# Load order of the down weights, place of the norm row, and order of the mixer's last group in a two-layer streaming encoder

## The chip, the cores and the metric

The kernel runs on one core of one Trainium2 chip. The metric is the device time of one execution in microseconds (us). A core has TensorE (matrix products), VectorE, ScalarE and GpSimd (elementwise work), and SyncE, whose queue here issues nearly all transfers. In rows they are PE, DVE, ACT, POOL and SP. The engines run on their own and meet at semaphores. PSUM is the memory that TensorE writes to; all other tiles are in SBUF.

## The reference

Two layers over 1024 prompt frames and 8 x 16 sample frames, taken together as T = 1152 rows of 1024 numbers. All is float32.

```python
def _rmsnorm(x, g):
    y = xf * lax.rsqrt(jnp.mean(xf * xf, axis=-1, keepdims=True) + EPS)
    return y * g
def _swiglu(h, w_gu, w_down):
    gate, up = jnp.split(h @ w_gu, 2, axis=-1)
    return (jax.nn.silu(gate) * up) @ w_down
def _trunk(x, ...):
    for layer in range(2):
        h = _rmsnorm(x, norm[layer])
        y = _ab_mixer(h, ...) if layer == 0 else attention(h @ c_w_qkv) @ c_w_out   # mixer ends in o @ ab_w_out
        x = x + y
        x = x + _swiglu(_rmsnorm(x, ffn_norm[layer]), ffn_w_gu[layer], ffn_w_down[layer])
    return _rmsnorm(x, final_norm)
```

w_gu is 1024 x 5632, w_down is 2816 x 1024, c_w_qkv is 1024 x 3072.

## The kernel before

x stands transposed in SBUF as `xT`: 8 tiles (n = 0 to 7) of 128 features by 1152 frames. Every float32 factor is split in a high part (a cast, on ScalarE) and a low part (the difference, on VectorE or GpSimd), and a product is three matrix products: high by high, high by low, low by high.

**The pair products.** The two wide projections into the feed-forward (22 tile pairs each) and the projection to q, k, v (12 pairs) form each pair of output tiles by seven block products instead of eight. For pair p, product q (0 to 6) takes four token blocks (`token_block`, made once) and one weight block (`w_block`), which is 4 x 6 = 24 matmuls (`block_product`, L780). `PairWeights.make_sums` (GpSimd, L745 to L750, four instructions) forms the weight sums of a pair, `high_part` (ScalarE, L757) and `low_part` (GpSimd, L761) split each block. GpSimd makes the four sums of pair p, then the seven low parts in order. TensorE waits for the low part of a block before the product. The token blocks of products 3 to 6 are made late, beside the first pair (p = 0): four instructions each for the high part (`high_late`, L602 and L604, ScalarE) and the low part (L609 and L614, VectorE). The sums of pair 1 overwrite parts of `xT`, so GpSimd first waits until the last low part of product 6 is made (`tok.wait_late(pool, 6)`).

**The norm row.** 1 / rms of a frame multiplies the results of the products, not their inputs. TensorE sums the squares (`norm.sums`, L466), ScalarE takes the root (`norm.root`, L483), VectorE inverts (`norm.invert`, L495), TensorE spreads the 9 x 128 values over the partitions with 9 matmuls (`spread_group`, L476) in the middle of the first pair, and ScalarE copies the three groups to `norm_row` (`keep_group`, L488). Pair 1 and the results of pair 0 wait for them. This first pair exists three times: in the feed-forward of layer 0, in the q, k, v projection, and in the feed-forward of layer 1. In the last two the weight blocks of products 4 and 5 are also made late: their low parts come after the late low parts of token blocks 4 (`tok.wait_late(pool, 4)`).

**The down product.** `silu(gate) * up` of each pair (an `act_slot`, high and low, 1152 KB) goes to DRAM and comes back when SBUF is free. The product with w_down runs in three rounds of 8 units (u = 0 to 23), a unit being one output tile n over the slots of its round: 6 slots in the first round of both feed-forwards (54 matmuls, L1095). `load_unit(u)` (L880) waits for the split of unit u - 2, `split_down` on GpSimd (L968, L970) waits for the weights and for unit u - 2 on TensorE, the add into `xT` is on VectorE (L1326). Slots 6 to 13 are for the second round, which starts at u = 8. The SP queue issues in program order; an issue that waits holds up all behind it.

**The end of the mixer.** `mixer_out` multiplies by ab_w_out in three groups of 384 frames; the last group (`LAST`) has 8 products (L3975, 24 matmuls each). After each, VectorE adds into `xT` (L4048), ScalarE squares (L4003), and for every second tile i the token blocks are begun: `keep_x` saves the tile to DRAM, `scale` (L551) multiplies by the gain, `high_x11`, `high_t1`, `high_t2` (L555, L559, L563) on ScalarE and `make_t1`, `low_x11`, `make_rest`, `low_t` (L567, L572, L580 to L586, L593) on VectorE. TensorE then starts with product 0 of the first feed-forward pair, which needs `low_x11` of i = 0 to 3, and products 1 and 2; a barrier between two stages follows.

## Time and profile before

| | us |
|---|---|
| median of 3 runs | 3313.23 |
| lowest, highest | 3306.69, 3318.53 |
| the profiled execution, its own time | 3311.18 |
| its span, first to last instruction | 3309.5 |
| TensorE busy in it | 3123.8 (94%) |
| VectorE, ScalarE, GpSimd busy | 1484.4, 990.5, 1460.2 |
| mean granted TensorE clock | 0.974 of full |

The trace is of one execution. A wait is idle time of an engine put down to the instruction that released it. "PEclk" is the granted TensorE clock: 1.00 is 2.4 GHz, 0.50 is 1.2 GHz.

### The profile page before, as it was taken

How to read it: one execution, taken by the hardware profiler on the slowest of the kernel's cores; microseconds unless marked ns; L12 is line 12 of the kernel's file. 1: busy time of each engine (PE TensorE's matmuls, PEld its weight loads, DVE VectorE, ACT ScalarE, POOL GpSimd, SP SyncE). 2: the span in 40 equal slices, each digit the busy share in tenths (PEclk: the TensorE clock that was granted, in tenths of full speed). 3: DMA queues.
4: the chain of work that ended last, by engine and by line, in shares of the span. 5: the costliest groups of instructions: out<-in, count | busy, mean ns of one | idle time of the engine just before them, and what ended most of it. 6: DMA issues, size and time to landing. Idle time of an engine off the chain costs nothing. (4 is left out here: it accounts for less than half of the span.)

```text
span 3309.5 us, 66573 instructions
## 1 busy us (share of the span) xinstructions
PE 3123.8 (94%) x28370; PEld 2933.2 (89%) x28370; DVE 1484.4 (45%) x2051; ACT 990.5 (30%) x1744; POOL 1460.2 (44%) x1102
## 2 busy tenths in 40 slices
PE   7999978888897999997999999999999999998998
PEld 6988856777897999997999999777799999998997
DVE  5650044656665555442115433466646455451112
ACT  4212132334434233230003422266524333330003
POOL 4452144433315776772323655211136766762232
PEclk8999988999998999999999999999999999999999
DMA  6322141433741232238321343466522333237321
GB/s 203 84 89 86 48 135 63 142 123 110 228 156 58 96 109 94 99 106 327 135 80 70 98 152 125 170 200 221 150 76 81 103 104 99 96 129 282 131 81 58
DMA packets 379653, 413.61 MB, mean 125 GB/s; under 512 B 27832, under 2 KB 322321, under 8 KB 378344
## 3 DMA queue, kind: packets, MB, share of 16 engines
q1 hardware_dynamic: 375400, 394.65, 35.9%
q0 software_dynamic: 3968, 14.81, 1.5%
q8 instruction: 221, 3.62, 0.5%
q14 instruction: 64, 0.52, 0.1%
HBM read 274.54 MB, written 136.96 MB: 124 GB/s over the span
## 5 line engine op out<-in xcount | busy, mean ns | idle before, releaser
L780 PE MATMUL PS<-token_block,w_block 128*128 128x288 f32 x9408 | 1264.6, 296 | 12.7 <-DVE token_block L572 7.8
L780 PEld LDWEIGHTS PS<-token_block,w_block 128*128 128x128 f32 x9408 | 1257.8, 189 | 14.6 <-DVE token_block L572 8.1
L1095 PE MATMUL PS<-act_slot,w_down_split 128*128 128x384 f32 x3024 | 533.0, 338 | 29.2 <-POOL w_down_split L970 29.2
L1095 PEld LDWEIGHTS PS<-act_slot,w_down_split 128*128 128x128 f32 x3024 | 532.0, 189 | 29.8 <-POOL w_down_split L970 29.8
L761 POOL TENSOR_TENSOR w_block<-w_pair_raw,w_block 128x512 fp32r<-128x512 f32 x224 | 295.2, 1321 | 175.1 <-ACT w_block L757 135.3
L761 POOL TENSOR_TENSOR w_block<-w_sum,w_block 128x512 fp32r<-128x512 f32 x168 | 217.2, 1309 | 105.0 <-ACT w_block L757 105.0
L1326 DVE TENSOR_TENSOR xT<-xT,PS 128x1152 f32<-128x1152 f32 x48 | 65.0, 1354 | 430.9 <-PE PS L1095 423.1
L757 ACT CAST w_block<-w_pair_raw 128x512 fp32r<-128x512 f32 x224 | 138.1, 620 | 286.4 <-PE PS L780 271.1
L968 POOL CAST w_down_split<-w_down_raw 128x768 fp32r<-128x768 f32 (+2 forms) x48 | 44.8, 933 | 405.7 <-PE PS L1095 311.5
L757 ACT CAST w_block<-w_sum 128x512 fp32r<-128x512 f32 x168 | 99.4, 620 | 364.4 <-POOL w_sum L750 225.4
L745 POOL TENSOR_TENSOR w_sum<-w_pair_raw 128x512 f32<-128x512 f32 x56 | 90.5, 1617 | 159.1 <-DMA w_pair_raw<-in_ffn_w_gu_dram 111.9
L405 PE MATMUL PS<-hT_high,w_split_tiles 128*128 128x384 f32 x576 | 125.4, 344 | 2.8 <-DVEq L2200 2.8
L747 POOL TENSOR_TENSOR w_sum<-w_sum,w_pair_raw 128x512 f32<-128x512 f32 x56 | 118.9, 2123 | 4.4
L1293 DVE TENSOR_TENSOR u<-p,PS 128x576 f32<-128x576 f32 x44 | 33.1, 753 | 182.9 <-PE PS L780 182.9
L405 PEld LDWEIGHTS PS<-hT_high,w_split_tiles 128*128 128x128 f32 x576 | 101.9, 191 | 3.1 <-POOLq L2070 3.1
L4381 ACT ACTIVATE probs<-minus_scores,minus_max 128x640 f32<-128x640 f32 (+3 forms) x144 | 101.1, 705 | 12.2 <-DVE minus_max L4451 12.2
L970 POOL TENSOR_TENSOR w_down_split<-w_down_raw,w_down_split 128x768 fp32r<-128x768 f32 (+2 forms) x48 | 101.8, 2120 | 3.8
L1307 DVE TENSOR_TENSOR ffn_up<-ffn_up,norm_row 128x1152 f32<-128x1152 f32 x44 | 99.6, 2264 | 4.6
L2864 POOL TENSOR_TENSOR gla_k_exps<-gla_exps,gla_kT 128x896 f32<-128x896 f32 x18 | 37.0, 2079 | 145.6 <-ACT gla_exps L3284 145.6
L4419 POOL COPY bias_samples<-bias_near 128x384 f32<-128x384 f32 x16 | 8.0, 502 | 188.0 <-DMA bias_near<-near_dram 164.6
L4451 DVE CUSTOM_DVE_ANT_0 minus_scores<-PS,bias_pair 128x640 f32<-128x640 f32 (+4 forms) x128 | 79.2, 655 | 25.8 <-PE PS L4274 25.5
L405 PE MATMUL PS<-hT,w_split_tiles 128*128 128x384 f32 x504 | 89.3, 339 | 0.0
(448 smaller groups left out, 5064.7 us busy)
## 6 DMA issues: line engine op xcount, KB each, us to landing
act_slot<-act_dram SPq DMA_DIRECT2D x44, 1152.0 KB, 11.6
w_pair_raw<-in_ffn_w_gu_dram SPq DMA_DIRECT2D x88, 512.0 KB, 5.2
act_dram<-ffn_act_high SPq DMA_DIRECT2D x44, 576.0 KB, 2.8
act_dram<-ffn_act_low SPq DMA_DIRECT2D x44, 576.0 KB, 3.9
cache_kT<-kT_dram SPq DMA_DIRECT2D x8, 2048.0 KB, 11.7
cache_v<-in_cache_c_v_dram SPq DMA_DIRECT2D x64, 256.0 KB, 4.8
xT<-xT_dram SPq DMA_DIRECT2D x24, 576.0 KB, 10.3
w_pair_raw<-in_c_w_qkv_dram SPq DMA_DIRECT2D x24, 512.0 KB, 5.0
```

Source lines behind the costliest of these rows:

```text
L405: m = nc.tensor.matmul(PS[:, banks + j, 0:GN], wl if p == 2 else wh, sl if p == 1 else sh, start=(k == first and p == 0), stop=(k == last ...
L745: tt(self.sum_(p, 2), b0, b1, ALU.add).then_inc(self.summed, 1)
L747: tt(self.sum_(p, 1), self.sum_(p, 2), a0, ALU.subtract).then_inc(self.summed, 1)
L757: self.nc.scalar.copy(self.blocks[q][:, 0], self.source(p, q)).then_inc(self.high, 1)
L761: self.nc.gpsimd.tensor_tensor(self.blocks[q][:, 1], self.source(p, q), self.blocks[q][:, 0], ALU.subtract).then_inc(self.low, 1)
L780: m = nc.tensor.matmul(to[:, j], w, x[:, j * HN:(j + 1) * HN], start=(q < 3 and i == 0 and t == 0), stop=(q > 3 and i == 3 and t == 2), sk ...
L970: nc.gpsimd.tensor_tensor(wd[s][:, 1, k], wd_raw[s][:, k], wd[s][:, 0, k], ALU.subtract).then_inc(wd_low, 1)
L1095: m = nc.tensor.matmul(down_banks(u)[:, j], wd[u % 2][:, int(q == 2), k], x[:, int(q == 1), group(j)], start=(k == 0 and q == 0), stop=(k ...
L1307: tt(up[:], up[:], row[:], ALU.mult).then_inc(up_scaled, 1)
L1326: tt(groups(xT[:, n]), groups(xT[:, n]), down_banks(u), ALU.add).then_inc(x_added, 1)
L4381: nc.scalar.activation(pr[:, g % 2, hp, 0:w], sc[:, hp, 0:w], ACT.Exp, scale=-1.0, bias=mn[:, g % 2, hp, 0:1], accum_out=sm[:, g % 2, hp, ...
L4451: v.tensor_tensor_reduce(sc[:, hp, 0:w], x, b, -1.0, -NEG, ALU.add, ALU.min, mn[:, g % 2, hp, 0:1]).then_inc(score_max[hp], 1)
```

## The change

Three edits that do not touch each other. No instruction is added or removed.

1. SP queue, both feed-forwards: slots 6 to 13 and (layer 0) the first q, k, v weights were issued before unit 4's weights; now units 4 to 7 are each followed by two slots, and the q, k, v weights come after unit 8's.
2. All three first pairs: the spread of the norm row moves from after product 3 to after product 4; the root, the inversion and the three copies move on ScalarE and VectorE.
3. Mixer, last group: adds and squares are interleaved with the token blocks one by one.

```diff
@@ ffn_in_seven, sync
         sp.wait_ge(mm, done(NP - 1, 6))
-        for j in range(6, 14):
-            load_slot(j)
...
-        if follow:
-            follow.wts.load(sp, 0)
         for u in range(4, NU):
             load_unit(u)
+            if u < 8:
+                load_slot(2 * u - 2)
+                load_slot(2 * u - 1)
+            if u == 8 and follow:
+                follow.wts.load(sp, 0)
@@ first_pair, tensor (the same in qkv_in_seven)
             product(0, 3, range(4))
-            spread_all()
             pe.wait_ge(p1_kept, 1)
             pe.wait_ge(wts.low, wts.count(0, 4))
             product(0, 4, range(4))
+            spread_all()
@@ scalar (the same in qkv_in_seven)
         keep_p1(0)
+        norm.root(act)
         for i in range(4):
             tok.high_late(act, 4, i)
         for q in wts.order[5:7]:
             wts.high_part(act, 0, q)
         for i in range(4):
             tok.high_late(act, 5, i)
-        norm.root(act)
+        for j in range(G):
+            norm.keep_group(act, j)
         act.wait_ge(wts.low, 7)
         for i in range(4):
             tok.high_late(act, 6, i)
-        for j in range(G):
-            norm.keep_group(act, j)
@@ vector (the same in qkv_in_seven)
         early(0)
+        norm.invert(dve)
         for i in range(4):
             tok.low_x_late(dve, 4, i)
         middle(0)
         for i in range(4):
             tok.low_t_late(dve, 5, i)
-        norm.invert(dve)
@@ mixer_out, scalar, last group
             square(LAST, 2 * i)
-            square(LAST, 2 * i + 1)
             act.wait_ge(x_squared, LAST * KT + 2 * i + 1)
             tok.scale(act, i)
             tok.high_x11(act, i)
             tok.high_t1(act, i)
+            square(LAST, 2 * i + 1)
             tok.high_t2(act, i)
@@ mixer_out, vector, last group
+        add(LAST, 1)
         for i in range(4):
-            if i:
-                add(LAST, 2 * i)
-            if i < 3:
-                add(LAST, 2 * i + 1)
             tok.make_t1(dve, i)
             tok.low_x11(dve, i)
-            if i == 3:
+            if i < 3:
+                add(LAST, 2 * i + 2)
+            else:
                 add(LAST, 7)
             dve.wait_ge(added, LAST * KT + 2 * i + 2)
             tok.make_rest(dve, i)
+            if i < 2:
+                add(LAST, 2 * i + 3)
             tok.low_t(dve, 2, i)
             tok.low_t(dve, 1, i)
```

On the SP queue, in the feed-forward of layer 0 after the last loads of `xT`, there stood before (`act_slot_11967` to `_11974` are slots 6 to 13, L880 loads the down weights of units 4, 5, ..., L736 the first q, k, v weights):

```order
L884 DMA act_slot_11967<-act_dram 128x2x1152
L884 DMA act_slot_11968<-act_dram 128x2x1152
L884 DMA act_slot_11969<-act_dram 128x2x1152
L884 DMA act_slot_11970<-act_dram 128x2x1152
L884 DMA act_slot_11971<-act_dram 128x2x1152
L884 DMA act_slot_11972<-act_dram 128x2x1152
L884 DMA act_slot_11973<-act_dram 128x2x1152
L884 DMA act_slot_11974<-act_dram 128x2x1152
L736 DMA w_pair_raw_11940<-in_c_w_qkv_dram 128x8x128 x2
L880 DMA w_down_raw<-in_ffn_w_down_dram 128x6x128
L880 DMA w_down_raw_11976<-in_ffn_w_down_dram 128x6x128
```

and there stands now:

```order
L880 DMA w_down_raw<-in_ffn_w_down_dram 128x6x128
L884 DMA act_slot_11967<-act_dram 128x2x1152
L884 DMA act_slot_11968<-act_dram 128x2x1152
L880 DMA w_down_raw_11976<-in_ffn_w_down_dram 128x6x128
L884 DMA act_slot_11969<-act_dram 128x2x1152
L884 DMA act_slot_11970<-act_dram 128x2x1152
L880 DMA w_down_raw<-in_ffn_w_down_dram 128x6x128
L884 DMA act_slot_11971<-act_dram 128x2x1152
L884 DMA act_slot_11972<-act_dram 128x2x1152
L880 DMA w_down_raw_11976<-in_ffn_w_down_dram 128x6x128
L884 DMA act_slot_11973<-act_dram 128x2x1152
```

The weights of unit 4 move ahead of all eight slots, those of units 5, 6 and 7 behind two, four and six of them.

On ScalarE, in the first pair of layer 0's feed-forward, there stood before, from the last late high part of product 5 on (`token_block_2750` to `_2753` are product 6's, L757 is the first block of pair 1):

```order
L602 CAST token_block_2749<-xT 128x576
L483 ACTIVATE norm_by_token<-PS,norm_eps_11902 128x9
L604 ACTIVATE token_block_2750<-xT,gains 128x576
L604 ACTIVATE token_block_2751<-xT,gains 128x576
L604 ACTIVATE token_block_2752<-xT,gains 128x576
L604 ACTIVATE token_block_2753<-xT,gains 128x576
L488 COPY norm_row<-PS 128x384 x3
L757 CAST w_block<-w_pair_raw 128x512
```

and there stands now:

```order
L602 CAST token_block_2749<-xT 128x576
L488 COPY norm_row<-PS 128x384 x3
L604 ACTIVATE token_block_2750<-xT,gains 128x576
L604 ACTIVATE token_block_2751<-xT,gains 128x576
L604 ACTIVATE token_block_2752<-xT,gains 128x576
L604 ACTIVATE token_block_2753<-xT,gains 128x576
L757 CAST w_block<-w_pair_raw 128x512
```

The three copies, which wait for TensorE's spread, now stand ahead of the high parts of product 6; the root has gone further up, behind `keep_p1`.

On VectorE, in the mixer's last group, there stood before, from the second instruction of i = 0 on (L4048 is the add; after the change it is L4049):

```order
L572 TENSOR_TENSOR token_block<-xT,token_block 128x576
L580 SCALAR_TENSOR_TENSOR token_sum<-xT,gains,token_sum_2758 128x576
L583 SCALAR_TENSOR_TENSOR xT<-xT,gains 128x576
L586 SCALAR_TENSOR_TENSOR xT<-xT,gains,token_sum 128x576
L593 TENSOR_TENSOR token_block_2734<-token_sum_2758,token_block_2734 128x576
L593 TENSOR_TENSOR token_block_2730<-token_sum,token_block_2730 128x576
L4048 TENSOR_TENSOR xT<-xT,PS 128x384 x2
L567 TENSOR_TENSOR token_sum_2759<-xT 128x576
L572 TENSOR_TENSOR token_block_2727<-xT,token_block_2727 128x576
L580 SCALAR_TENSOR_TENSOR token_sum_2755<-xT,gains,token_sum_2759 128x576
```

and there stands now:

```order
L572 TENSOR_TENSOR token_block<-xT,token_block 128x576
L4049 TENSOR_TENSOR xT<-xT,PS 128x384
L580 SCALAR_TENSOR_TENSOR token_sum<-xT,gains,token_sum_2758 128x576
L583 SCALAR_TENSOR_TENSOR xT<-xT,gains 128x576
L586 SCALAR_TENSOR_TENSOR xT<-xT,gains,token_sum 128x576
L4049 TENSOR_TENSOR xT<-xT,PS 128x384
L593 TENSOR_TENSOR token_block_2734<-token_sum_2758,token_block_2734 128x576
L593 TENSOR_TENSOR token_block_2730<-token_sum,token_block_2730 128x576
L567 TENSOR_TENSOR token_sum_2759<-xT 128x576
L572 TENSOR_TENSOR token_block_2727<-xT,token_block_2727 128x576
L4049 TENSOR_TENSOR xT<-xT,PS 128x384
```

The two adds that stood together behind all the work of i = 0 now stand inside it, the first ahead of L580 and the second ahead of L593.

## Rows read from the trace of the kernel before

**Rows 1.** Waits of TensorE over the whole span: us in total, times, longest.

```profile
PE PS L1095 <- POOL w_down_split L970: 29.2, 2, 17.6
...
PE PS L476 <- DVE norm_by_token L495: 13.6, 3, 4.8
...
PE PS L780 <- DVE token_block L572: 7.8, 1, 7.8
```

**Rows 2.** Timeline of the SP queue, first down stage: start us, us, line, count.

```profile
1536.73 10.74 SPq L884 DMA_DIRECT2D act_slot<-act_dram  x8
```

**Rows 3.** Timeline of GpSimd, first down stage, same columns, idle time before.

```profile
1569.75 0.82 POOL L968 CAST w_down_split<-w_down_raw 128x768 fp32r<-128x768 f32 x1 [30.64 <-DMA w_down_raw<-in_ffn_w_down_dram]
```

**Rows 4.** Timeline of VectorE, adds after down units, first and second down stage.

```profile
1555.00 1.35 DVE L1326 TENSOR_TENSOR xT<-xT,PS 128x1152 f32<-128x1152 f32 x1 [8.01 <-PE PS L1095]
1584.07 1.35 DVE L1326 TENSOR_TENSOR xT<-xT,PS 128x1152 f32<-128x1152 f32 x1 [27.71 <-PE PS L1095]
...
3026.57 1.35 DVE L1326 TENSOR_TENSOR xT<-xT,PS 128x1152 f32<-128x1152 f32 x1 [8.15 <-PE PS L1095]
3050.76 1.35 DVE L1326 TENSOR_TENSOR xT<-xT,PS 128x1152 f32<-128x1152 f32 x1 [22.84 <-PE PS L1095]
```

**Rows 5.** Windows: us, busy time by engine, PEclk (granted clock), DMA share, GB/s.

```profile
2988.00:3026.00 38.00, 38.00 (x218) 38.00 (x218) 8.29 (x7) 2.32 (x2) 5.34 (x4) 1.00 1.00 386
1831.00:1836.00 5.00, 5.00 (x23) 5.00 (x24) 2.81 (x4) 1.87 (x5) 2.04 (x2) 0.50 0.41 108
```

**Rows 6.** Timeline of TensorE, end of the mixer stage.

```profile
1006.17 1.81 PE L780 MATMUL PS<-token_block,w_block 128*128 128x288 f32 x6 [7.84 <-DVE token_block L572]
1010.41 6.40 PE L780 MATMUL PS<-token_block,w_block 128*128 128x288 f32 x36 [2.43 <-issue]
```

**Rows 7.** Timeline of VectorE and of ScalarE, last mixer group.

```profile
978.18 1.43 DVE L593 TENSOR_TENSOR token_block<-token_sum,token_block 128x576 fp32r<-128x576 f32 x2 [0.46 <-DVE xT L586]
979.53 1.01 DVE L4048 TENSOR_TENSOR xT<-xT,PS 128x384 f32<-128x384 f32 x2
...
987.09 3.41 DVE L593 TENSOR_TENSOR token_block<-token_sum,token_block 128x576 fp32r<-128x576 f32 x2
...
982.04 1.26 ACT L551 ACTIVATE xT<-xT,gains 128x1152 f32<-128x1152 f32 x1 [0.94 <-DMA xT_dram<-xT]
```

**Rows 8.** Timeline of TensorE, first pair of the projection after the first feed-forward.

```profile
1821.22 2.06 PE L466 MATMUL PS<-consts_f,norm_row 128*128 128x1 f32 x18
1823.14 3.42 PE L780 MATMUL PS<-token_block,w_block 128*128 128x288 f32 x24
1831.00 4.21 PE L476 MATMUL PS<-consts_f,norm_by_token 128*128 128x128 f32 x18 [4.43 <-DVE norm_by_token L495]
1834.87 13.57 PE L780 MATMUL PS<-token_block,w_block 128*128 128x288 f32 x96
```

**Rows 9.** Timeline of ScalarE, same place.

```profile
1828.40 2.76 ACT L604 ACTIVATE token_block<-xT,gains 128x576 fp32r<-128x576 f32 x4
...
1845.26 0.62 ACT L757 CAST w_block<-w_sum 128x512 fp32r<-128x512 f32 x1 [2.58 <-PE PS L780]
```

**Rows 10.** Timeline of VectorE, same place.

```profile
1830.87 2.94 DVE L614 SCALAR_TENSOR_TENSOR token_block<-xT,gains,token_block 128x576 fp32r<-128x576 f32 x4
```

**Rows 11.** Timeline of GpSimd, same place.

```profile
1825.34 2.51 POOL L761 TENSOR_TENSOR w_block<-w_pair_raw,w_block 128x512 fp32r<-128x512 f32 x2 [15.83 <-DVE token_block L614]
1833.88 1.29 POOL L745 TENSOR_TENSOR w_sum<-w_pair_raw 128x512 f32<-128x512 f32 x1 [6.03 <-DVE token_block L614]
...
1839.01 1.30 POOL L761 TENSOR_TENSOR w_block<-w_pair_raw,w_block 128x512 fp32r<-128x512 f32 x1
```

**Rows 12.** Timeline of GpSimd and of ScalarE, first pairs of the first feed-forward.

```profile
1044.62 5.45 POOL L761 TENSOR_TENSOR w_block<-w_pair_raw,w_block 128x512 fp32r<-128x512 f32 x3
...
1055.92 1.32 POOL L745 TENSOR_TENSOR w_sum<-w_pair_raw 128x512 f32<-128x512 f32 x1 [4.59 <-DMA w_pair_raw<-in_ffn_w_gu_dram]
...
1046.89 0.62 ACT L757 CAST w_block<-w_sum 128x512 fp32r<-128x512 f32 x1 [2.57 <-PE PS L780]
```

More of the change, by code:

```diff
@@ L1812, in first_pair @@
             product(0, 3, range(4))
-            for j in range(G):
-                norm.spread_group(pe, j)
             pe.wait_ge(p1_kept, 1)
@@ L1817, in first_pair @@
             product(0, 4, range(4))
+            for j in range(G):
+                norm.spread_group(pe, j)
             pe.wait_ge(u3_done, 1)
@@ L1899, in scalar @@
         keep_p1(0)
+        norm.root(act)
         for i in range(4):
@@ L1905, in scalar @@
             tok.high_late(act, 5, i)
-        norm.root(act)
+        for j in range(G):
+            norm.keep_group(act, j)
         act.wait_ge(wts.low, 7)
@@ L1909, in scalar @@
             tok.high_late(act, 6, i)
-        for j in range(G):
-            norm.keep_group(act, j)
         for q in range(6):
@@ L1984, in vector @@
         early(0)
+        norm.invert(dve)
         for i in range(4):
@@ L1989, in vector @@
             tok.low_t_late(dve, 5, i)
-        norm.invert(dve)
         for i in range(4):
```

## The prediction

> **What bounds the kernel now.** I read the page first: TensorE is busy 94% of the span, so only its idle time and its slow stretches can be won. The waits of TensorE come next [rows 1]. Three kinds belong to the three edits: 29.2 us in two waits for split down weights, 13.6 in three for the inverted norm, 7.8 in one for a token block. Last come the timelines of the engines around each, and windows for the granted clock [rows 5]: behind such a wait TensorE works for some microseconds at 0.50, the 1.2 GHz level, so a wait costs more than its idle time.
>
> **Down weights.** In the first down stage SP begins at 1536.73 to issue the eight slots, unit 4's weights stand behind them [rows 2], and GpSimd splits these at 1569.75 after 30.64 us of waiting for them [rows 3]. The full price is in the distance of VectorE's adds. Undisturbed, two lie 8.01 + 1.35 = 9.36 us apart; here it is 1584.07 - 1555.00 = 29.07, so 19.7 are lost, 17.6 of them idle and 2.1 at the low clock. In the second stage the undisturbed distance is 8.15 + 1.35 = 9.50, here 3050.76 - 3026.57 = 24.19, so 14.7 are lost [rows 4]. Together 34.4 us.
>
> After the change the next thing that could be late is units 5, 6 and 7, each behind two slots more. Two slots are 2.30 MB, a unit of six tiles is 0.39 MB; at the 386 GB/s of the busy stretch [rows 5] that is 6.0 + 1.0 = 7.0 us for each unit of 9.36. At the start up to three loads of xT (1.8 MB) are ahead: unit 4 lands about 1536.7 + 5.6 = 1542, unit 5 about 1549. GpSimd may split unit 4 when unit 2 is done, one unit before the add of 1555.00, at 1545.6, and unit 5 at 1555.0. So both are there 4 us early, and each later one gains 2 us. SP now waits between the pairs of slots, for a split each, and the last pair goes out near 1559 and lands by 1575; it is read from unit 8 on, at 1555 + 4 x 9.4 = 1592. Behind SP's waits stand only later weights, which need the same splits. The q, k, v weights are read after all units. I cost these moves at nothing; without that cover a wait of some microseconds a unit comes back. Term: -34.4, bounds -24 (two units of each stage 2.5 us late) and -34.4.
>
> **Mixer, last group.** After its last products TensorE waits 7.84 us for the low part of the last x11, then 2.43 for weight blocks [rows 6]. VectorE made adds 2 and 3 at 979.53 without waiting: product 2 had long ended. ScalarE's scale of i = 1, at 982.04, waited for the save of that tile, which needs the add [rows 7]. Inside the work of i = 0, add 2 can go at 975.5 and that scale near 979. Part of the lead is lost again: add 3 now waits for product 3 (ended about 979.2, a product being 4.2 us), add 5 for product 5, and later pieces meet GpSimd's sums: two L593 took 3.41 us there, against 1.43 at 978.18 [rows 7]. Followed piece by piece in this way, the last low x11 is ready near 1001 instead of 1006.1: -5. The weight blocks move with it, since ScalarE makes them behind the same pieces, so the 2.43 stays. The 36 matmuls took 6.40 us [rows 6], by the rate of the first pair 36 x 3.42 / 24 = 5.1 [rows 8]; some of these 1.3 us may go. Term: -6, bounds 0 (the pieces just as late) and -7.8 - 1.3 = -9.1.
>
> **Norm row.** In the q, k, v pair TensorE waits 4.43 us ahead of the spread, and the spread and the start of product 4 run at 0.50 [rows 5, 8]. From the end of product 3 (1823.14 + 3.42 = 1826.6) to that of product 6 (ScalarE's next block, released by it, starts at 1845.26) it is 18.7 us [rows 8, 9]. The work inside is products 4 to 6, 3.2 us each, and the spread, 3.87 at the low clock (1831.00 to 1834.87) and half of it, 1.9, at best; I take 2.1. So 11.7 would do: the edit looks worth 7 us a place, 21 in all.
>
> What comes instead is read from what stands behind the three copies. Before, the high parts of product 6 ran at 1828.40, ahead of the spread, their low parts at 1830.87, and GpSimd's first sum of pair 1 at 1833.88 waited for these [rows 9 to 11]. Now the copies, which wait for the spread, stand ahead of the high parts. From the end of the spread: the last copy 0.5 us, four high parts 2.8, the last low part 0.8, together 4.1. Then GpSimd's four sums and the first low part of pair 1, 1833.88 to 1839.01 + 1.30: 6.4 us [rows 11]. VectorE will then be busy with the results of pair 0; where it is, three L761 take 5.45 us instead of 3 x 1.3, 1.6 more [rows 12]. That is 12.1 us from the end of the spread to the start of pair 1, and products 5 and 6 fill 6.4: a new wait of 5.7 us at the head of pair 1 in each of the three places. Before, the block was there at 1840.3, 5 us ahead of TensorE.
>
> The root is late too. It now holds ScalarE until the sums end (1821.22 + 2.06 = 1823.3) [rows 8], about 2.5 us later than the high parts of product 4 began, and their last low part comes 2 us later than the 1825.3 at which it released GpSimd's blocks for products 4 and 5 [rows 11]. With 1.3 us for the block, product 4 starts at 1828.7, 2.1 us after product 3. In layer 1's first pair it is the same; in layer 0 that block is made early, so 0.
>
> The sum for the q, k, v pair: 2.1 + 3.2 (product 4) + 2.1 (spread) + 12.1 = 19.5, before 18.7, so +0.8. After a wait of that length the first 5 us of work are at half rate [rows 5], +2.5. So +3.3 there and in layer 1, +1.2 in layer 0. Term: +8, bounds -21 (GpSimd's chain not on the path) and +15 (the low clock ahead of product 4 as well, twice 2 us, and VectorE costing GpSimd 1.6 us more in two of the places).
>
> The Trainium skill, page SBUF — State Buffer, section SBUF: two separate sides, states that a VectorE instruction with two SBUF inputs and a GpSimd instruction that reads SBUF exclude each other, the one that comes second being blocked for the whole of the other. It speaks against this edit, which moves GpSimd's sums beside VectorE's results; the 3.41 us of the two L593 agree with it, and it is worked out as rival C. By the lack of such a rule (GpSimd at its bare 6.4 us) the sum would be 5 us lower.
>
> **The sum.** 3311.2 (the execution's own time) - 34.4 - 6 + 8 = 3278.8. The median of the runs shown is 2 us above that execution; half of it put on gives 3280 us.
>
> **Rivals.**
> A, the norm edit pays. If the first block of pair 1 were not late: 3311 - 34 - 6 - 21 = 3250. For it the visible 13.6 us; against it that GpSimd's sum waited for a token block of product 6, and these now come behind the copies.
> B, the transfers change places only. Units 5 to 7 come late behind their slots and two thirds of the gain go: 3280 + 23 = 3303. For it a DMA share of 1.00 in that stretch; against it 7.0 us of data for each 9.36 us.
> C, GpSimd is blocked longer. Its chain at the head of pair 1 is five instructions, not three, and VectorE has more results waiting: twice the 1.6 us in all three places, 3280 + 5 = 3285. For it the 3.41 us; against it 5.45 us for three, which is less than a block of each.
> D, slower: lateness is handed on. Pair 1 of layer 0 began at 1046.89, and pair 2's first sum came 9.0 us later, at 1055.92, behind its weights [rows 12]. These are loaded after the sixth block of pair 1, which now is made after pair 1 begins: the first sum about 14 us after the start, the first block at 21 to 22, needed at 22.4 and the 2.5 of the low clock. From 0.6 us of wait in every one of the 53 pairs (21 + 11 + 21) the gain is eaten; at 0.8 it is 3280 + 42 = 3322. Against it: from pair 3 on blocks follow TensorE's own products, and 10 us are to spare.
>
> **Chances.** Forecast 0.65, A 0.12, C 0.12, B 0.08, D 0.03. The forecast's own terms end at 3312 - 34 - 9 + 2 = 3271 and at 3312 - 31 - 2 + 15 = 3294. Half of A's way is possible, a wait that is there but short, so the range starts at 3260; it ends at 3294. Some 0.3%, 10 us, is what a measurement of this kernel can tell from no change. Faster: the forecast, A, C and a third of B, 0.92. Within 0.3%: the rest of B, 0.05. Slower: D, 0.03.
>
> **What would show it.** No wait of TensorE for down weights, and adds 9.36 and 9.50 us apart over the first nine units; the wait for the inverted norm gone; three new waits at the first product of pair 1, released by GpSimd's L761, 4 to 8 us each, with a clock of 0.50 behind them; two of about 2 us ahead of product 4; the mixer's wait for a token block down to 1 to 4 us. I am wrong if pair 1 starts without a wait (A), if down units still wait for weights (B), or if waits stand in later pairs (D).

## The result, and the profile after

| | before | after |
|---|---|---|
| median of the timed runs | 3313.23 us (11 runs) | 3293.42 us (11 runs) |
| profiled execution: its time / its span | 3311.2 / 3309.5 us | 3293.16 / 3291.5 us |
| ratio after : before | | 0.9947, 95% interval 0.9930 to 0.9964 |

The change makes the kernel 17.6 us faster by the ratio, 20 by the medians; 33 were forecast, and the time lies inside the range of 3260 to 3294 only just. The numbers of lines after L930 are one or two higher than before.

First TensorE's waits, the view that answers to [rows 1] (us in total, times, longest):

```profile
PE PS L780 <- POOL w_block L761: 21.6, 4, 6.1
...
PE PS L780 <- issue: 5.5, 3, 2.9
```

No line for down weights is left, and none for the inverted norm. The wait for GpSimd's w_block was not there before: it is three waits of 6 us at the head of pair 1 and one of 3.5 ahead of product 4 in layer 1. The wait ahead of product 4 in the q, k, v pair is booked under "issue". Where they stand, the timeline of TensorE shows; this is layer 1's first pair (start us, us, engine, line, instruction, count, idle time before and its releaser):

```profile
2482.84 2.06 PE L466 MATMUL PS<-consts_f,norm_row 128*128 128x1 f32 x18
2484.76 3.42 PE L780 MATMUL PS<-token_block,w_block 128*128 128x288 f32 x24
2491.71 4.94 PE L780 MATMUL PS<-token_block,w_block 128*128 128x288 f32 x24 [3.52 <-POOL w_block L761]
2496.45 2.44 PE L476 MATMUL PS<-consts_f,norm_by_token 128*128 128x128 f32 x18
2498.64 6.49 PE L780 MATMUL PS<-token_block,w_block 128*128 128x288 f32 x48
2511.27 18.93 PE L780 MATMUL PS<-token_block,w_block 128*128 128x288 f32 x121 [6.14 <-POOL w_block L761]
```

The spread (L476) now follows product 4 without a wait and takes 2.44 us. But product 4 waits 3.52 us, takes 4.94 instead of 3.42, and pair 1 waits 6.14. In the q, k, v pair products 3 and 4 read:

```profile
1802.99 4.96 PE L780 MATMUL PS<-token_block,w_block 128*128 128x288 f32 x24
1809.93 4.94 PE L780 MATMUL PS<-token_block,w_block 128*128 128x288 f32 x24 [1.97 <-issue]
```

Product 3 is at the low clock there and takes 1.5 us more, and the wait behind it is shorter by as much: from start to start it is 6.94 us, as in layer 1 (6.95). In both places product 4 so starts 3.52 us after a product 3 of 3.42 us would have ended. Before, the same place in the q, k, v pair had one wait of 4.43 [rows 8]. Windows of the two stretches behind layer 1's waits show the granted clock (us, busy time by engine, clock, DMA share, GB/s):

```profile
2492.00:2496.00 4.00, 4.00 (x23) 4.00 (x22) 3.48 (x4) 0.53 (x1) 0.85 (x1) 0.64 0.44 124
2512.00:2516.00 4.00, 4.00 (x19) 4.00 (x19) 0.20 (x1) 3.74 (x5) 4.00 (x4) 0.50 0.00 0
```

The 0.64 is a mean: in windows of 1 us the clock is still 1.00 from 2491.8 to 2492.8, 0.50 from 2493.8 to 2495.8, and on its way up behind that.

ScalarE in layer 1's pair says why product 4 is late, the first three rows; the fourth is the first of the copies, the fifth the high parts of product 6 behind them:

```profile
2484.98 1.28 ACT L483 ACT_TABLE_LOAD   x1 [4.14 <-PE PS L466]
2486.28 0.27 ACT L483 ACTIVATE norm_by_token<-PS,norm_eps 128x9 f32<-128x9 f32 x1
2486.45 2.76 ACT L604 ACTIVATE token_block<-xT,gains 128x576 fp32r<-128x576 f32 x4
...
2497.36 0.48 ACT L488 COPY norm_row<-PS 128x384 f32<-128x384 f32 x1 [4.83 <-PE PS L476]
...
2499.30 2.78 ACT L604 ACTIVATE token_block<-xT,gains 128x576 fp32r<-128x576 f32 x4
```

ScalarE waited 4.14 us for the sums, and only then loaded the root's activation table, 1.28 us. GpSimd's blocks, their low parts and pair 1's sums follow, answering to [rows 11]:

```profile
2490.33 2.52 POOL L761 TENSOR_TENSOR w_block<-w_pair_raw,w_block 128x512 fp32r<-128x512 f32 x2 [16.12 <-DVE token_block L614]
2503.20 1.29 POOL L745 TENSOR_TENSOR w_sum<-w_pair_raw 128x512 f32<-128x512 f32 x1 [10.34 <-DVE token_block L614]
2504.57 2.46 POOL L747 TENSOR_TENSOR w_sum<-w_sum,w_pair_raw 128x512 f32<-128x512 f32 x1
...
2509.95 1.27 POOL L761 TENSOR_TENSOR w_block<-w_pair_raw,w_block 128x512 fp32r<-128x512 f32 x1
```

In the down stages VectorE's adds, which answer to [rows 4], are the first two rows from layer 0, the last two from layer 1:

```profile
1554.55 1.35 DVE L1327 TENSOR_TENSOR xT<-xT,PS 128x1152 f32<-128x1152 f32 x1 [8.01 <-PE PS L1096]
1563.91 1.35 DVE L1327 TENSOR_TENSOR xT<-xT,PS 128x1152 f32<-128x1152 f32 x1 [8.01 <-PE PS L1096]
...
3022.53 1.35 DVE L1327 TENSOR_TENSOR xT<-xT,PS 128x1152 f32<-128x1152 f32 x1 [8.15 <-PE PS L1096]
3032.03 1.35 DVE L1327 TENSOR_TENSOR xT<-xT,PS 128x1152 f32<-128x1152 f32 x1 [8.14 <-PE PS L1096]
```

They are 9.36 and 9.50 us apart, with no gap. The SP queue issues unit 4 at 1536.08, the pairs of slots at 1536.50, 1539.11, 1548.47 and 1557.83, as the order says.

At the end of the mixer TensorE's waits, which answer to [rows 6], are:

```profile
1004.34 1.34 PE L780 MATMUL PS<-token_block,w_block 128*128 128x288 f32 x6 [4.17 <-DVE token_block L572]
1008.57 6.44 PE L780 MATMUL PS<-token_block,w_block 128*128 128x288 f32 x36 [2.88 <-issue]
```

**Where the time went, by marks on TensorE.** Three stretches, each cut by the same instructions in every kernel: layer 0's first sums (L466) to its first down unit; the sums of the q, k, v pair to those of layer 1; these to layer 1's first down unit. Each holds one norm row and otherwise nothing that was edited. Four kernels hold the norm row as before (the kernel before, e1, e3, e7); their sums over the three are 1662.6, 1665.7, 1666.1 and 1662.5 us, mean 1664.2. After: 496.8 + 681.8 + 501.5 = 1680.1, so the norm edit costs 15.9 us. The sums of these four differ by up to 3.6 us, so a difference of 2 us in them says little. The first down stage took 294.3 and takes 274.6 (-19.7), the second 267.6 and 253.5 (-14.1). The mixer's end, from the scale of i = 0 (ScalarE L551) to the sums, took 49.15 and takes 45.2 (-3.9). Together -21.8, where the spans differ by -18.0. Of the 4 us between, 1.6 is the distance of the first kernel's own 1662.6 from the mean, and 2.2 had come up by the first L551 of the mixer's last group (972.78 and 974.94), ahead of all that was edited; see below.

### The profile page after: what moved, and what is told of

It reads as the page before. It is cut to its first block and busy times, and to the rows that moved or that the text cites. A ratio compares the mean times of both kernels' runs of the same rounds, so it can differ in the third digit from the quotient of the medians.

```text
span 3291.5 us, 66575 instructions
## 1 busy us (share of the span) xinstructions
PE 3127.2 (95%) x28370; PEld 2935.7 (89%) x28370; DVE 1488.1 (45%) x2051; ACT 989.3 (30%) x1744; POOL 1463.8 (44%) x1102
## 5 line engine op out<-in xcount | busy, mean ns | idle before, releaser
L761 POOL TENSOR_TENSOR w_block<-w_pair_raw,w_block 128x512 fp32r<-128x512 f32 x224 | 294.9, 1320 | 179.7 <-ACT w_block L757 131.4
L761 POOL TENSOR_TENSOR w_block<-w_sum,w_block 128x512 fp32r<-128x512 f32 x168 | 217.8, 1313 | 104.3 <-ACT w_block L757 104.3
L757 ACT CAST w_block<-w_pair_raw 128x512 fp32r<-128x512 f32 x224 | 137.5, 619 | 291.0 <-PE PS L780 266.4
L757 ACT CAST w_block<-w_sum 128x512 fp32r<-128x512 f32 x168 | 99.3, 620 | 369.4 <-POOL w_sum L750 233.9
L1318 DVE TENSOR_TENSOR ffn_gate<-ffn_gate,ffn_up 128x1152 f32<-128x1152 f32 x44 | 60.3, 1370 | 68.2 <-ACT ffn_gate L1171 68.2
```

The lines of the kernel that those rows point to most:

```text
L757: self.nc.scalar.copy(self.blocks[q][:, 0], self.source(p, q)).then_inc(self.high, 1)
L761: self.nc.gpsimd.tensor_tensor(self.blocks[q][:, 1], self.source(p, q), self.blocks[q][:, 0], ALU.subtract).then_inc(self.low, 1)
```

## The experiments

All times are medians of the timed runs, ratios to the kernel before on the same chip. "Three stretches" is the sum just defined.

**e1, the down edit alone** (the norm row and the mixer as before):

```diff
...
+            if u < 8:
+                load_slot(2 * u - 2)
+                load_slot(2 * u - 1)
...
```

> The kernel before with the first edit alone (slots queued between pairs). Theory: the edit is worth its forecast 34.4 us by itself, as the marks in the two down stages of the changed kernel say (19.7 and 14.7 us), and touches nothing else: 3313 - 34 = 3279 us, ratio 0.9896. Rival: the edit has a cost elsewhere (the first part of the changed kernel and other untouched stages came out 3.9 us longer in its profile), and this would be it: 3283 us, ratio 0.991. Rival 2: part of the 34 us is only won together with the other edits: above 3287 us.

Measured: 3283.43 us, ratio 0.9909 (0.9883 to 0.9935), in its profile the down stages take 274.6 and 253.5 us. The edit is worth its 34 locally; the ratio's 30 has that inside its interval. The first rival (a cost elsewhere) can't be excluded by the time, but no wait in the profile speaks for it.

**e2, the norm row's edit alone:**

> The kernel before with the second edit alone (norm row: spread one product later, root and reciprocal earlier, copies earlier). Theory formed after the result: the edit costs 16 us, 1.4 in layer 0, 6.8 in the q, k, v pair and 8.3 in layer 1: 3313 + 16 = 3329 us, ratio 1.005. The term as predicted: +8, 3321 us, ratio 1.0024. Rival A of the prediction: -21, 3292 us.

Measured: 3330.99 us, ratio 1.0061 (1.0037 to 1.0085). The three stretches sum to 1680.7, +16.5. The edit makes the kernel slower by itself, by twice what was forecast, and the term as predicted (1.0024) is outside the interval.

**e3, the mixer's edit alone:**

> The kernel before with the third edit alone (mixer's last group interleaved). Theory: the wait for the low part of x11 at the end falls from 7.84 to 1.3 us, the one for weight blocks rises from 2.43 to 6.4, and 4 us are won: 3309 us, ratio 0.9988. The term as predicted: -6, 3307 us. VectorE's L583 and L586 beside GpSimd's sums: 1.5 us each as in the changed kernel, against 0.8 before.

Measured: 3311.15 us, ratio 0.9990 (0.9968 to 1.0011): the total can't tell it from nothing. The stretch from L551 to the sums can: 49.2, 49.6 and 49.6 us in the three kernels without the edit, 45.2 to 46.0 in the ten that have it and nothing else new there (46.0 here), mean 45.7. So -3.7 us. The two waits did not come out as expected: in e3 the wait for the low x11 is 3.86 us (7.84 before, 1.3 expected) and the one for the weight blocks 2.42 (2.43 before, 6.4 expected). L583 and L586 take 1.57 each, as expected.

**e7, the change without the norm row's edit:**

> The changed kernel with the norm row's edit undone in all places (first and third edit stay). Theory (the norm edit costs 16 to 18 us): 3293 - 17 = 3276 us, ratio to before 0.9888. The term as predicted (+8): 3285 us. If the norm edit cost nothing: 3293.

Measured: 3279.16 us, ratio 0.9874 (0.9847 to 0.9902), 14 us below the change by the medians. Leaving out one of its three edits makes the change better.

**e12 and e11: which step of the norm edit costs what.** e12 puts root and reciprocal back and keeps the rest:

```diff
-        norm.root(act)
         for i in range(4):
             tok.high_late(act, 4, i)
...
         for i in range(4):
             tok.high_late(act, 5, i)
+        norm.root(act)
         for j in range(G):
             norm.keep_group(act, j)
```

> The changed kernel with root and reciprocal put back to where they stood before (copies early, spread late, as changed). Theory: no wait ahead of product 4 in any place; a wait of about 1.2 us at the spread for the reciprocal; waits of 5.5 to 7 us at pair 1, released by GpSimd, as in the changed kernel: 3293 - 8 = 3285 us. If the early root alone were at fault for pair 1 too: waits there under 2 us, 3273 us.

Measured: 3284.44 us, ratio 0.9905 (0.9885 to 0.9925), three stretches 1671.8, +7.6. TensorE in layer 1:

```profile
2479.69 6.62 PE L780 MATMUL PS<-token_block,w_block 128*128 128x288 f32 x48
2487.55 2.50 PE L476 MATMUL PS<-consts_f,norm_by_token 128*128 128x128 f32 x18 [1.23 <-DVE norm_by_token L495]
2489.80 6.64 PE L780 MATMUL PS<-token_block,w_block 128*128 128x288 f32 x48
2502.43 27.79 PE L780 MATMUL PS<-token_block,w_block 128*128 128x288 f32 x197 [5.99 <-POOL w_block L761]
```

As expected: products 3 and 4 run as one, the spread waits 1.23 us, pair 1 waits 5.99. So the late spread with the early copies costs 7.6 us in all, and the early root the other 8.3. In layer 1 the spread starts 9.8 us after the sums here and 13.6 in the change.

e11 puts only the copies back behind the high parts of product 6:

> The changed kernel with the three copies of the norm row put back behind the high parts of product 6 (root and reciprocal early, spread late, as changed). Theory (the early root makes everything behind it in the first pair late, the copies add to it at pair 1): the waits ahead of product 4 stay at 2 to 3.5 us (q, k, v and layer 1); at pair 1 the sums no longer wait for the copies but for the weights' load behind blocks 5 and 6, so the waits fall from 6 us to 1 to 2 us: 3293 - 14 = 3279 us. If the copies alone were at fault at pair 1: waits there 0, 3275 us. If they weren't: 3293 us.

Measured: 3284.06 us, ratio 0.9903 (0.9883 to 0.9923). Ahead of product 4 TensorE waits 3.52 and 3.51 us in the q, k, v pair and layer 1, at pair 1 it waits 3.47, 1.15 and 0.88 instead of 6 (layer 0 more than expected). With e12 the theory holds: each part alone leaves waits, neither alone is the fault. (The three stretches of e11 can't be compared: its last one ran at another pace, see the end.)

**e8, the activation table loaded during the wait:**

```diff
     def root(self, act):
         act.wait_ge(self.eps_set, 1)
+        self.nc.scalar.activation(self.eps[:, 1:2], self.eps[:, 0:1], ACT.Sqrt)
         act.wait_ge(self.summed, 1)
```

> The changed kernel with one more instruction on ScalarE: a square root of one column of a constant, ahead of the root's wait for the sums, so that the activation table is loaded during that wait. Theory (the table load of 1.28 us runs only after the wait and stands on the path to product 4): the wait ahead of product 4 falls by 1.3 us in the q, k, v pair and in layer 1, that of layer 0 is unchanged (no table load there); the waits at pair 1 stay, since they count from the spread: 3293 - 2 x 1.3 = 3290 us, to 3287 if the clock comes back earlier too. Rival (the low clock ahead of product 4 has another cause, and the table load is hidden): nothing moves.

Measured: 3293.90 us, ratio 0.9933 (0.9916 to 0.9951): no change that a time can show, and the three stretches (1677.8) are 2.3 shorter, about their scatter. But the steps are as expected. ScalarE and TensorE in layer 1:

```profile
2486.65 1.28 ACT L482 ACT_TABLE_LOAD   x1
2487.95 0.20 ACT L482 ACTIVATE norm_eps<-norm_eps 128x1 f32<-128x1 f32 x1
2490.72 0.27 ACT L484 ACTIVATE norm_by_token<-PS,norm_eps 128x9 f32<-128x9 f32 x1 [2.57 <-PE PS L466]
```

```profile
2496.15 4.95 PE L781 MATMUL PS<-token_block,w_block 128*128 128x288 f32 x24 [2.18 <-issue]
```

The wait ahead of product 4 is 2.18 instead of 3.52, 1.34 less, and 2.1 was the value forecast without the table. The q, k, v pair has 2.18 as well. The low clock behind it (4.95 us for the product) is the same.

**e4, root later and copies back** (the part that shows where the root stands now; the copies stand behind the high parts of product 6):

```diff
...
         for q in wts.order[5:7]:
             wts.high_part(act, 0, q)
+        norm.root(act)
         for i in range(4):
             tok.high_late(act, 5, i)
...
```

> The changed kernel with the norm row's small steps put elsewhere: root behind the high parts of product 4 and of the weight blocks 5 and 6 (the reciprocal behind the VectorE work of product 3), the copies back behind the high parts of product 6; the spread stays behind product 4. Theory (the waits come from ScalarE held by root, with its table load, and by the copies, and from nothing else): no wait of TensorE ahead of product 4, at the spread or at pair 1 over 1 us in any of the three places; the norm row gives -18 to -21 instead of +16: 3313 - 34 - 4 - 20 = 3255 us, ratio 0.9825. Rival (GpSimd's sums of pair 1 are late whatever stands ahead of them, since it is slower beside VectorE's results): waits of 3 to 6 us at pair 1 stay, 3275 us or more. Rival 2 (inverting is late for the spread): a wait of 1 to 3 us at the spread, 3262 us.

Measured: 3277.51 us, ratio 0.9906 (0.9881 to 0.9931), three stretches 1660.5, -3.7. The theory half fell. Nothing waits over 0.2 us ahead of product 4 or at the spread, but the 13.6 us of before did not turn into 18 to 21 of gain: TensorE comes to pair 1 sooner and waits there, 3.59, 2.49 and 3.54 us. VectorE and GpSimd in layer 1:

```profile
2483.75 3.00 DVE L614 SCALAR_TENSOR_TENSOR token_block<-xT,gains,token_block 128x576 fp32r<-128x576 f32 x4
```

```profile
2486.83 1.29 POOL L745 TENSOR_TENSOR w_sum<-w_pair_raw 128x512 f32<-128x512 f32 x1 [6.68 <-DVE token_block L614]
```

The sums of pair 1 start when product 6's last low part is made, 12.7 us after TensorE's sums, as they did before (2507.86 - 2495.19); the early chain of TensorE can't pull them.

**e5 and e6: let the sums start sooner.** Both ease one wait of GpSimd, e5 in the change, e6 in e4:

```diff
-        tok.wait_late(pool, 6)
+        tok.wait_late(pool, 5, 2)
```

> The changed kernel with one wait of GpSimd eased in each of the three places: its sums for pair 1 wait for the third token block of product 5 (the last one whose storage they overwrite) and not for the last of product 6; nothing else is moved. Theory (the wait of 6 us at pair 1 is the chain copies, high parts of product 6, their low parts, GpSimd's sums): all three waits at pair 1 fall under 1 us and the low clock behind them goes: 3293 - 3 x (6.0 + 2.3) = 3268 us. The two waits ahead of product 4 (2.0 and 3.5 us) stay. Rival C (GpSimd beside VectorE is what is slow): the sums then take 8 us wherever they stand, but start 9 us sooner, so the wait goes all the same; it would show only as sums of 8 instead of 5 us. Rival D (lateness is handed on to pair 2): a wait of 1 to 3 us turns up at pair 2, and the gain is 15 us, 3278.

Measured: 3286.28 us, ratio 0.9917 (0.9899 to 0.9934), three stretches 1668.8, 11 below the change where 25 were expected. The waits of 6 us at pair 1 are gone (only layer 1 keeps one, 1.31), but product 6 itself now waits for its low parts, seven times in the three places, 4.9 us together, and in layer 0 TensorE waits another 2.36 us for a result of VectorE ("DVE u L1289") in pair 1. VectorE and GpSimd in layer 1:

```profile
2493.69 6.11 DVE L614 SCALAR_TENSOR_TENSOR token_block<-xT,gains,token_block 128x576 fp32r<-128x576 f32 x4 [3.11 <-ACT token_block L604]
```

```profile
2493.78 1.89 POOL L745 TENSOR_TENSOR w_sum<-w_pair_raw 128x512 f32<-128x512 f32 x1 [5.82 <-DMA w_pair_raw<-in_ffn_w_gu_dram]
2495.74 1.68 POOL L747 TENSOR_TENSOR w_sum<-w_sum,w_pair_raw 128x512 f32<-128x512 f32 x1
2497.38 1.80 POOL L748 TENSOR_TENSOR w_pair_raw<-w_pair_raw 128x512 f32<-128x512 f32 x1
```

The low parts take 6.11 us instead of 3.00, GpSimd's sums 1.7 to 1.9 each instead of 1.29. Rival C had GpSimd's side of this; that VectorE is slowed too, and makes product 6 late, was not expected: what is put side by side slows both. A second bound shows in the first POOL row: the sums waited for pair 1's weights, whose load waits for the blocks of L761 in pair 0.

> The kernel of e4 (late root, copies back) with the same easing of GpSimd's wait. e4 had no wait ahead of product 4 and at the spread, but waits of 3.59, 2.49 and 3.54 us at pair 1 for GpSimd's blocks, and 2.12 us behind them at the turns of the q, k, v stage. Theory (what held e4 is the start of GpSimd's sums alone): all four go: 3277 - 9.6 - 2.1 - 2 (low clock) = 3263 us, and it is the fastest of all. Rival: pair 2's weights then set the pace, a wait of 1 to 2 us in pair 2 of each place, 3268 us.

Measured: 3274.10 us, ratio 0.9878 (0.9858 to 0.9898), three stretches 1658.3, -5.9. Waits at pair 1 of 2.33, 2.27 and 3.00 us stay, where 0 was expected: in the q, k, v pair and layer 1 the sums now wait 5.8 us for the weights.

**e9, that load sooner too:** ScalarE's high parts of blocks 5 and 6 ahead of those of product 4, and GpSimd's wait ahead of their low parts taken out.

> The kernel of e6 with the last two weight blocks of pair 0 made sooner: ScalarE's high parts of blocks 5 and 6 stand ahead of the high parts of product 4, and GpSimd no longer waits for product 4's token blocks before their low parts. In e6 pair 1's weights (whose load waits for these blocks) were issued 5.4 us after product 3's start and landed 5.8 us behind the blocks; GpSimd's sums began on that landing in the q, k, v pair and layer 1 and TensorE waited 2.27 and 3.00 us for them, in layer 0 2.33. Theory (the bound of pair 1 is the ring blocks 5 and 6, load of the next weights, sums): the load starts about 5 us sooner, the sums then wait for product 5's token block only, and begin 3 us sooner in these two places; their waits fall to 0 to 0.8 us, and the 0.57 at the turns goes. Layer 0, whose sums waited for the token block, keeps its 2.3. 3274 - 5.3 - 1.5 (low clock) - 0.6 = 3267 us. Rival (VectorE and GpSimd slow each other when side by side, so what is started sooner ends no sooner): waits of 2 us stay, 3274 us.

Measured: 3272.94 us, ratio 0.9867 (0.9844 to 0.9889), the lowest median of all; three stretches 1661.1, -3.1. The time is nearer to the rival's. No wait for GpSimd is left in the three places, but VectorE is late instead: TensorE waits 2.35 and 2.41 us for its results ("DVE u L1288") inside pair 1 of the two layers. VectorE and GpSimd in layer 1:

```profile
2485.64 7.13 DVE L614 SCALAR_TENSOR_TENSOR token_block<-xT,gains,token_block 128x576 fp32r<-128x576 f32 x4
```

```profile
2485.13 1.72 POOL L745 TENSOR_TENSOR w_sum<-w_pair_raw 128x512 f32<-128x512 f32 x1 [6.87 <-DVE token_block L609]
...
2488.58 1.81 POOL L748 TENSOR_TENSOR w_pair_raw<-w_pair_raw 128x512 f32<-128x512 f32 x1
2490.34 1.81 POOL L750 TENSOR_TENSOR w_sum<-w_pair_raw,w_sum 128x512 f32<-128x512 f32 x1
```

Four low parts take 7.13 us and the sums 7.0, where they take 3.0 and about 5.1 alone. Between e6, e7 and e9 the intervals overlap, so which of them is best stays open; each beats both kernels.

**e10, the mixer with small sums:**

```diff
-            acc = e.norm_row[:, group(LAST)]
-            nc.gpsimd.tensor_tensor(acc, acc, part[:, n % 2], ALU.add).then_inc(sq_added, 1)
+            acc = e.norm_row[:, group(LAST)][:, 0:1]
+            nc.gpsimd.tensor_tensor(acc, acc, part[:, n % 2, 0:1], ALU.add).then_inc(sq_added, 1)
```

> The changed kernel with GpSimd's seven additions of the last group's squares cut to one column each (the sums over the other columns are left out). Question: why the mixer's wait fell by 3.8 and not by 6 us. Theory (VectorE's steps beside these additions take twice as long): L583 and L586 fall from 1.57 to 0.82 us each in the work of i = 0 and i = 2, L567 and L572 of i = 2 from 1.85 to about 1, and the last low part of x11 is ready 3 us sooner: the wait for it falls from 4.17 to about 1.2 us, unless the products bound the rest. About 3 us of 3293, 3290; the trace decides. Rival (the pieces are late because add 3 and add 5 wait for their products): durations of L583 and L586 stay, and so does the wait of 4.2 us.

This kernel leaves out the sums of all columns but one, and serves only to time the rest. Measured: 3290.69 us (0.9924, 0.9898 to 0.9950), which alone can't be told from the change; from L551 to the sums 43.0 us instead of 45.7, and the wait for the low x11 is 1.8 instead of 4.2. VectorE in the work of i = 0, first in the change, then here:

```profile
978.80 1.57 DVE L583 SCALAR_TENSOR_TENSOR xT<-xT,gains 128x576 f32<-128x576 f32 x1
980.30 1.56 DVE L586 SCALAR_TENSOR_TENSOR xT<-xT,gains,token_sum 128x576 f32<-128x576 f32 x1
```

```profile
975.37 0.81 DVE L583 SCALAR_TENSOR_TENSOR xT<-xT,gains 128x576 f32<-128x576 f32 x1
976.10 0.81 DVE L586 SCALAR_TENSOR_TENSOR xT<-xT,gains,token_sum 128x576 f32<-128x576 f32 x1
```

L583 and L586 are back at 0.81, as the theory said. L567 and L572 of i = 2 stay at 1.84 each: these stand beside the sums of the weights, which were not cut, so that part of the expectation was wrong.

## Why the prediction was half right, point by point

**Down weights, -34.4: right.** -33.8 in the change, -33.9 in e1, no wait, the adds 9.36 and 9.50 us apart as worked out. Nothing was lost to the transfers (rival B).

**Mixer, -6: the mechanism right, the size off by 2.3.** -3.7 over ten kernels. The pieces were followed with the durations that stood in the rows of before, but moved pieces have new neighbours: the adds of the squares now run beside L583 and L586. I had counted the meeting only for the L593. e10 gives 2.7 us back when these sums are small. That is as much as was missing, but partly by chance: of the 6 forecast, about 1 was to come from the 36 matmuls behind the wait, and these are as slow as before (6.44 us, before 6.40), while the wait itself fell by 3.7 us of the 5 forecast.

**Norm row, +8: this is the step that failed.** It measured +15.9 in the change, +16.5 alone, at the bound of +15 within the scatter of the three stretches. It had two halves, and the runs part them.

The late spread and the early copies were sized well: "a new wait of 5.7 us at the head of pair 1 in each of the three places" is 6.00, 5.99 and 6.14, at a clock of 0.50. GpSimd's chain from the first sum to the first block took 8.0 us in all three places, as forecast (6.4 + 1.6), so rival C, which had another 1.6 to come, is out. With the root left in its place these steps cost 7.6 (e12).

The sentence that failed is "with 1.3 us for the block, product 4 starts at 1828.7, 2.1 us after product 3". It starts 3.52 us after, in both places. I let ScalarE's high parts begin the moment the sums end, with nothing for the root. In fact the table load of 1.28 us comes first, and e8, which moves just that into the idle time, measures 2.18. Before, the load of the q, k, v pair began at 1826.94, and the reciprocal started only at 1830.74, when VectorE was done with other low parts: nobody waited for the load, so it had shown no price.

The second part was in the bounds, not in the value: product 4 runs at the low clock behind that wait, 4.94 instead of 3.42 us, in both places; up to the spread that is 4.8 us for the 3.2 of the sum. The third part is small: from the end of the spread to pair 1 it is 12.6 us in all three places (1816.86 to 1829.48 in the q, k, v pair), where the sum had 12.1. Wait and clock are 2 x (1.4 + 1.6) = 6.0, the chain 3 x 0.5 = 1.5, together 7.5 us of the 7.9 by which the term was off. The low clock behind pair 1 came as forecast (2.5): with 3.42 us for the first 24 matmuls and 0.1327 for each further one, layer 1's row has 18.93 - 3.42 - 97 x 0.1327 = 2.6 us too much, e12's 27.79 - 3.42 - 173 x 0.1327 = 1.4.

The Trainium skill, page ScalarE: Activation LUTs, section What ACT_TABLE_LOAD costs, gives about 1283 ns for such a load, and the trace agrees with 1.28 us. The page adds about 1380 ns of drain, 2.66 us for a switch in all; here the measurement decides against that: the root began 1.30 us after the load did (2484.98 and 2486.28). What neither it nor the rows of before told is where it goes when the instruction behind it waits.

**Rival A (the norm edit pays)** is out: e2 is slower than the kernel before. What is more, e4, e6 and e9 show that little of the visible 13.6 us of before could be had, in these three orders at least: with the waits for the norm row gone, the three stretches fall by 3.7, 5.9 and 3.1 us. TensorE then waits for GpSimd's blocks, or for VectorE. Before, in layer 1, the first block was ready 19.1 us after the start of L466 (2514.3 - 2495.2) and TensorE came for it at about 23.3 (the end of product 6 released ScalarE at 2518.5); a lead of 4 us was all there was to win in that place. In e4 the sums start at the same 12.7 us, but now beside VectorE's results, and the block is ready at 20.6: 1.6 of the lead is gone, and the low clock behind the wait takes 1.7 of the rest (30.44 us for 215 matmuls, reckoned as above).

**Rival D (handed on)** showed in a small way: waits of 2.1 us at the turns of the q, k, v stage in e4 and 2.8 in e9, none in later pairs.

**The contention rule.** In e9 a low part (0.75 us alone) and a sum (1.29 alone) come every 1.8 us, when both engines are busy all the time. The Trainium skill, page SBUF — State Buffer, section SBUF: two separate sides, says that of such two the one that starts second is blocked for the whole of the other; 0.75 + 1.29 = 2.04 would be that (an estimate from that rule and the rows), so the trace agrees but for 0.2 us of overlap. In the prediction I asked only what this does to GpSimd, behind the copies; the cost in e5 and e9 is on VectorE's side.

**Untouched places.** At the first L551 of the mixer's last group the profile of after is 2.2 us behind. From 230 to 260 us, where all kernels are alike, TensorE does 126 matmuls in the change and 133 before; e1 and e3, without the norm row's edit, also have 126, e4 and e12 134. Over all kernels that L551 starts between 971.5 and 980.6. So this is scatter of the execution, not the change.

## What to carry to other kernels

A wait on the busiest engine is worth at most the lead of the next thing behind it: look how early the next block is ready before you count the wait as a gain. When a step with a long input is moved to the front of an in-order engine, count everything behind its wait, a table load in front of it included, and put a one-column instruction of the same function into idle time if the load is on the path (1.34 us a place in e8, too little for the total to show). When VectorE work with two SBUF inputs is moved beside GpSimd work, size both with the duration they have side by side: in e9 1.8 us each, 2.4 times the 0.75 of the low part and 1.4 times the 1.29 of the sum.

## What the hardware showed that I had not expected

The granted clock behind a wait of the same length differs from run to run and place to place. In e5 both waits ahead of product 4 are 3.52 us; in layer 1 the product then takes 3.42 us at 1.00, in the q, k, v pair 6.10 at 0.50:

```profile
1810.00:1815.00 5.00, 5.00 (x21) 5.00 (x22) 3.62 (x4) 0.69 (x2) 1.00 (x1) 0.50 0.56 158
2487.00:2490.00 3.00, 3.00 (x24) 3.00 (x24) 3.00 (x4) 0.63 (x2) 0.96 (x1) 1.00 0.22 56
```

TensorE has two paces at the same granted clock. In e11's second feed-forward, and in no other of the windows that I read in the feed-forwards, it does 387 matmuls in 50 us, against 377 (e12, below it); the stage is 10 us shorter for it (483.4 us from sums to down, against 494.0, the mean of the four kernels with the norm row as before).

```profile
2600.00:2650.00 50.00, 50.00 (x387) 50.00 (x386) 24.74 (x24) 15.47 (x23) 37.73 (x27) 1.00 0.34 114
```

```profile
2600.00:2650.00 50.00, 50.00 (x377) 50.00 (x376) 24.68 (x22) 14.62 (x23) 36.75 (x26) 1.00 0.34 114
```

What sets the pace stays open. That profiled run of e11 took 3272.31 us, its other five 3282.5 to 3286.3. A run with one stage at the faster pace looks 10 us better than it is, as much as any edit of the norm row, so here marks around the edited place told more than the total.
